# A hybrid encoder layer: order of the recurrence's drains, banks by result in its chunk step, and the key norm's root and reciprocal on tokens by heads

## The reference

```python
h = rms_norm(x, pre_mix_g);  z = h @ w_in          # 2048 -> 7296 columns
ya = neighbourhood_attention(...)                  # 8 heads of 64
yb = rwkv7_mixer(...)                              # 12 heads of 64, both directions
yc = retention_mixer(...)                          # 6 heads of 128
x = x + rms_norm(concat(ya, yb, yc) @ w_out, post_mix_g)
x = x + rms_norm(square(relu(rms_norm(x, pre_mlp_g) @ w_up)) @ w_down, post_mlp_g)
```

```python
kk = k * k_k;  kk = kk / max(sqrt(sum(kk * kk over 64 channels)), 1e-12)
# per token, state 64 x 64 per head and direction
sa = state @ (-kk)
state = state * w + outer(sa, kk * a) + outer(v, kd);   y = state @ r
```

## Time and profile before

| | us |
|---|---|
| median of 3 runs | 1355.91 |
| the runs | 1347.48, 1356.33, 1355.91 |
| profiled execution, its own time | 1349.03 |
| its span, first to last instruction | 1347.2 |
| PE busy / DVE / ACT / POOL | 1293.1 / 837.8 / 650.2 / 308.1 |

### The profile page before, as it was taken

One profiled execution on the slowest core, in us unless ns is written; L12 is line 12 of the kernel. 1 busy time (PEld: TensorE's weight loads), 2 busy tenths in 40 slices (PEclk: granted clock), 3 DMA queues, 4 the chain that ended last, 5 costly groups with the idle time before them and its releaser, 6 DMA issues.

```text
span 1347.2 us, 25329 instructions
## 1 busy us (share of the span) xinstructions
PE 1293.1 (96%) x10465; PEld 1132.2 (84%) x10465; DVE 837.8 (62%) x1179; ACT 650.2 (48%) x992; POOL 308.1 (23%) x255
## 2 busy tenths in 40 slices
PE   6999999999999899998999999999999999999996
PEld 5999888888899888877888888888888888888885
DVE  5566788888885976547555555555555545555455
ACT  5465654566434446447444444444444444444443
POOL 0011333243305121000455544444430000000000
PEclk9999999999999999998999999999999999999999
DMA  8666433233349334764766666666666666666663
GB/s 258 182 171 176 121 97 97 80 82 94 108 109 214 103 110 126 261 223 125 225 192 191 189 189 189 191 192 191 190 189 195 194 191 196 191 191 198 190 195 116
DMA packets 285751, 226.44 MB, mean 168 GB/s; under 512 B 15236, under 2 KB 263300, under 8 KB 284740
## 3 DMA queue, kind: packets, MB, share of 16 engines
q1 hardware_dynamic: 285168, 223.57, 56.8%
q0 software_dynamic: 240, 1.18, 0.3%
q10 hardware_dynamic: 228, 0.07, 0.0%
HBM read 222.69 MB, written 2.10 MB: 167 GB/s over the span
## 4 chain that ended last, share of the span: by engine, by line
PE 83%; DVE 8%; ACT 5%; issue 3%; DMA 1%; ACTq 0%; DVEq 0%
PE psum L2086 31%; PE psum L1733 18%; PE psum L1734 9%; PE psum L1722 7%; PE psum L1723 6%; PE psum L1724 6%; DVE w_lo L777 2%; ACT w_hi L1327 1%; PE psum L1865 1%; DMA raw<-in_w_out 1%; PE psum L1850 1%; PE psum L1789 1%; PE psum L1928 0%; PE psum L2141 0%; DVE arena L851 0%
## 5 line engine op out<-in xcount | busy, mean ns | idle before, releaser
L777 DVE TENSOR_TENSOR w_lo<-raw,w_hi 128x1024 fp32r<-128x1024 f32 x394 | 495.0, 1259 | 402.2 <-ACT w_hi L1327 401.3
L1327 ACT ACTIVATE w_hi<-raw 128x1024 fp32r<-128x1024 f32 x394 | 418.8, 1066 | 457.6 <-PE psum L2086 213.3
L1733 PE MATMUL psum<-act_both,w_hi 128*128 128x512 f32 x1024 | 355.4, 394 | 0.0
L2086 PE MATMUL psum<-w_hi,act_both 128*128 128x512 f32 x1216 | 327.4, 390 | 4.5 <-DVE act_both L1280 2.7
L1734 PE MATMUL psum<-act_both,w_lo 128*128 128x256 f32 x1024 | 283.8, 277 | 0.0
L1722 PE MATMUL psum<-act_both,w_hi 128*128 128x256 f32 x912 | 271.6, 298 | 7.5 <-DVE w_lo L777 6.1
L2086 PEld LDWEIGHTS psum<-w_hi,act_both 128*128 128x128 f32 x1216 | 227.7, 188 | 53.3 <-DVE act_both L1280 3.1
L1723 PE MATMUL psum<-act_both,w_hi 128*128 128x256 f32 x912 | 258.1, 283 | 0.0
L1724 PE MATMUL psum<-act_both,w_lo 128*128 128x256 f32 x912 | 257.8, 283 | 0.0
L1733 PEld LDWEIGHTS psum<-act_both,w_hi 128*128 128x128 f32 x1024 | 192.0, 187 | 44.6 <-DVE w_lo L777 0.2
L1734 PEld LDWEIGHTS psum<-act_both,w_lo 128*128 128x128 f32 x1024 | 192.3, 188 | 0.0
(11 more groups left out here) (235 smaller groups left out, 1076.0 us busy)
## 6 DMA issues: line engine op xcount, KB each, us to landing
raw<-in_w_up SPq DMA_DIRECT2D x128, 512.0 KB, 4.1
raw<-in_w_down SPq DMA_DIRECT2D x128, 512.0 KB, 4.2
raw<-in_w_in SPq DMA_DIRECT2D x114, 512.0 KB, 4.3
raw<-in_w_out SPq DMA_DIRECT2D x32, 512.0 KB, 4.5
arena<-in_x SPq DMA_DIRECT2D x2, 1024.0 KB, 6.1
arena<-in_na_rpb SPq DMA_DIRECT2D x16, 128.0 KB, 4.7
arena<-in_x SPq DMA_DIRECT2D x1, 2048.0 KB, 10.8
out_x<-arena SPq DMA_DIRECT2D x4, 512.0 KB, 2.7
```

The lines of the kernel that those rows point to most:

```text
L777: dve.tensor_tensor(by_half(h, low(h)), by_pair(h, raw[:, h % RAW]), by_half(h, high(h)).bitcast(F32), ALU.subtract).then_inc(s["lo_half"], 1)
L1327: act.activation(by_half(h, high(h)), by_pair(h, raw[:, h % RAW]), ACT.Copy).then_inc(s["hi_half"], 1)
L1733: pe.matmul(bank[b].rearrange("p (a t) -> p a t", a=2), wh, act_both[:, :, kt], start=kt == 0, stop=False)
L2086: last = pe.matmul(bank[4 * t + 2 * j + b], lhs[:, tokens], w[:, b * 512:(b + 1) * 512], start=start, stop=stop)
```

## The change

- **Key norm.** The squares become the stationary operand and two columns of ones (one for each head) the moving one, so that the sums come out as 128 tokens by 2 heads, twice (256 tokens): four columns in place of 256. ACT's root, DVE's maximum and reciprocal (`kk_factor`, a step of its own) work on 128x4. Four matmuls with the factor column, broadcast to 64, as stationary operand and the identity as moving one spread the factors over each head's channels into unused columns of bank 5 (`kk_wide`); DVE's norm multiplies by that. `make_p` of level 0 waits for the norm, since both touch bank 5.
- **Chunk step.** Bank 0 holds g of both heads and bank 1 y of both. One ACT copy takes g, one ACT copy or one DVE addition takes y.
- **Levels.** DVE adds both directions, does its chunk step, and then transposes both (`turn_q`). On ACT the last level's inverse is drained ahead of `between` (the exponentials of direction 1).
- **Order and place.** The copy of the chunks' end decays goes from DVE to ACT (`again`), and ACT's `decays` waits for `again_ready`. On DVE the chunk's fourth step comes ahead of the norm; it is now empty there.

Cut out of the diff are the semaphores' names, `feed`'s list lengths, and repeated renamings of `gy[e]` to `g_ps` and `y_ps`.

```diff
@@ -206,6 +206,7 @@
         LORA_BANK = [2, 4]
+        kk_wide = bank[5].rearrange("p (a t) -> p a t", a=2)[:, :, P:T]
         scores = psum[:, 2:4].rearrange("p e (t k) -> p e t k", t=TT)
...
@@ -256,7 +257,7 @@
         bn = cut(X2 + 1792, T)
-        kk_ss = bn
+        kk_f = small[:, 244:244 + 2 * TT]
         tmp = cut(16640, T)
...
@@ -398,9 +399,9 @@
                 if t < RW_CT - 1:
-                    square, root, lora, norm = feed(t + 1)
+                    square, root, factor, lora, norm = feed(t + 1)
                     tl = tilde(t + 1, 1 - p)
-                    early = [(root,), (), (norm, lora), (tl[0],)]
+                    early = [(root,), (factor,), (lora, norm), (tl[0],)]
                     between = [(tl[1],), (), (), (), (tl[4],)]
...
@@ -435,7 +436,7 @@
         PE_STARTS = {15: "root", 19: "lora"}
-        STARTS = {12: "square", 18: "root", 20: "norm", 21: "lora", 26: "sums_0", 29: "keys_0",
+        STARTS = {12: "square", 17: "root", 18: "factor", 20: "norm", 21: "lora", 26: "sums_0", 29: "keys_0",
                   31: "sums_1", 33: "keys_1"}
...
@@ -826,16 +827,20 @@
             def feed(t):
+                def kk_factor():
+                    dve.wait_ge(s["kk_root"], t + 1)
+                    nxt(dve.tensor_scalar(kk_f, kk_f, 1e-12, None, ALU.max))
+                    dve.reciprocal(kk_f, kk_f).then_inc(s["kk_factor"], 1)
+
                 def kk_norm():
-                    dve.wait_ge(s["kk_root"], t + 1)
+                    dve.wait_ge(s["kk_spread"], t + 1)
                     dve.wait_ge(s["kb_ready"], 2 * t)
                     dve.wait_ge(s["query_ready"], 2 * t)
-                    nxt(dve.tensor_scalar(kk_ss, kk_ss, 1e-12, None, ALU.max))
-                    nxt(dve.reciprocal(kk_ss, kk_ss))
-                    dve.scalar_tensor_tensor(kkn, zk[:, t], small[:, 48 + t:49 + t], kk_ss, ALU.mult,
-                                             ALU.mult).then_inc(s["kk_ready"], 1)
-
-                return [nothing] * 3 + [kk_norm]
+                    dve.scalar_tensor_tensor(kkn.rearrange("p (a t) -> p a t", a=TT),
+                                             zk[:, t].rearrange("p (a t) -> p a t", a=TT), small[:, 48 + t:49 + t],
+                                             kk_wide, ALU.mult, ALU.mult).then_inc(s["kk_ready"], 1)
+
+                return [nothing, nothing, kk_factor, nothing, kk_norm]

...
@@ -860,8 +865,6 @@
                     dve.wait_ge(s["exp_ready"], 6 * t + (3 * d + 3))
-                    last_t = C - 1 if d == 0 else 0
-                    dve.tensor_copy(ec[p][:, d], chunks(e_inc)[:, :, last_t])
                     dve.wait_ge(s["kd_ready"], 2 * t + (d + 1))
...
@@ -924,8 +927,8 @@
                 gap()
+                steps[3]()
                 run(early[2])
-                steps[3]()
                 gap()
...
@@ -953,6 +956,10 @@
                     z_new = new_columns(zd[:, half], d, n)
                     dve.tensor_tensor(z_new, packed(q_ps, n), z_new, ALU.add).then_inc(s["zd_ready"], 1)
+
+                def turn_q(d):
+                    if n == len(LEVELS) - 1:
+                        return
                     dve.wait_ge(s["zd_ready"], 10 * t + (2 * (n + 1) + d + 1))
                     if d:
...
@@ -967,17 +974,15 @@
                 run(steps[1:])
+                turn_q(0)
+                turn_q(1)
                 gap()
...

-                gy = [bank[e][:, 0:2 * C].rearrange("p (d v) -> p d v", d=2) for e in range(2)]
+                g_ps, y_ps = (bank[e][:, 0:2 * C].rearrange("p (d v) -> p d v", d=2) for e in range(2))
                 both = slice(n, 2 * NC - n, 2 * NC - 1 - 2 * n)
-
-                def g():
-                    dve.wait_ge(s["gy_done"], 4 * b + (n + 1))
-                    dve.tensor_copy(gs[C:P], gy[1][C:P]).then_inc(s["g_high"], 1)

...
@@ -1007,14 +1012,13 @@
                     order = slice(NC - 1 - n, n + 1, 2 * n - NC + 1)
-                    dve.tensor_tensor(y_i[0:C, order], gy[1][0:C], y_i[0:C, order], ALU.add)
-                    dve.tensor_tensor(y_i[C:P, order], gy[0][C:P], y_i[C:P, order], ALU.add).then_inc(s["y_added"], 1)
+                    dve.tensor_tensor(y_i[:, order], y_ps, y_i[:, order], ALU.add).then_inc(s["y_added"], 1)

...

-                return g, u, state_and_y
+                return nothing, u, state_and_y

...
@@ -1390,8 +1394,8 @@
                     act.wait_ge(s["kk_summed"], t + 1)
-                    act.wait_ge(s["tilde_ready"], 2 * t)
-                    act.activation(kk_ss, bank[2][:, 0:T], ACT.Sqrt).then_inc(s["kk_root"], 1)
+                    act.wait_ge(s["kk_spread"], t)
+                    act.activation(kk_f, bank[2][:, 0:2 * TT], ACT.Sqrt).then_inc(s["kk_root"], 1)
                     if t == 0:
...
@@ -1423,6 +1427,7 @@
                     act.wait_ge(s["query_ready"], 2 * t + d)
+                    act.wait_ge(s["again_ready"], 2 * t + d)
                     if d == 1:
...
@@ -1433,6 +1438,11 @@
                     act.wait_ge(s["query_ready"], 2 * t + (d + 1))
+                    if t >= 2:
+                        act.wait_ge(s["dec_ready"], 2 * (t - 1))
+                        act.wait_ge(s["s_ready"], 3 * (t - 1))
+                    last_t = C - 1 if d == 0 else 0
+                    act.activation(ec[p][:, d], chunks(e_inc)[:, :, last_t], ACT.Copy)
                     for v in (ar[p][:, d], bk[:, d]):
...
@@ -1475,21 +1485,24 @@
                 gap()
-                run(between)
                 if n == len(LEVELS) - 1:
...
                     take_inverse(1)
-                run(steps[1:])
+                    run(steps[1:])
+                    run(between)
+                else:
+                    run(between)
+                    run(steps[1:])
                 gap()
...
             def chunk(b, q, n):
-                gy = [bank[e][:, 0:2 * C].rearrange("p (d v) -> p d v", d=2) for e in range(2)]
+                g_ps, y_ps = (bank[e][:, 0:2 * C].rearrange("p (d v) -> p d v", d=2) for e in range(2))
                 both = slice(n, 2 * NC - n, 2 * NC - 1 - 2 * n)
...
                     act.wait_ge(s["gy_done"], 4 * b + (n + 1))
-                    act.activation(gs[0:C], gy[0][0:C], ACT.Copy).then_inc(s["g_low"], 1)
+                    act.activation(gs, g_ps, ACT.Copy).then_inc(s["g_ready"], 1)

...
@@ -1502,8 +1515,7 @@
                     order = slice(n, NC - n, NC - 1 - 2 * n)
-                    act.activation(y_i[0:C, order], gy[1][0:C], ACT.Copy)
-                    act.activation(y_i[C:P, order], gy[0][C:P], ACT.Copy).then_inc(s["y_copied"], 1)
+                    act.activation(y_i[:, order], y_ps, ACT.Copy).then_inc(s["y_copied"], 1)

...
@@ -1757,7 +1769,19 @@
                     pe.wait_ge(s["lora_free"], 4 * t)
-                    pe.matmul(bank[2][:, 0:T], ones, kk_sq, start=True, stop=True).then_inc(s["kk_summed"], 1)
+                    for a in range(TT):
+                        last = pe.matmul(bank[2][:, 2 * a:2 * a + 2], kk_sq[:, a * P:(a + 1) * P], ones[:, 0::C],
+                                         start=True, stop=True)
+                    last.then_inc(s["kk_summed"], 1)
+
+                def spread():
+                    pe.wait_ge(s["kk_factor"], t + 1)
+                    for a in range(TT):
+                        for e in range(2):
+                            last = pe.matmul(kk_wide[e * C:e * C + C, a],
+                                             kk_f[:, 2 * a + e:2 * a + e + 1].broadcast_to([P, C]), ident, start=True,
+                                             stop=True)
+                    last.then_inc(s["kk_spread"], 1)

...
@@ -1772,8 +1796,9 @@
                     last.then_inc(s["lora_done"], 1)
-
-                return [nothing, kk_sum, lora, nothing]
+                    spread()
+
+                return [nothing, kk_sum, nothing, lora, nothing]

...
@@ -1844,6 +1869,8 @@
                     pe.wait_ge(s["zd_ready"], 10 * t + (2 * n + 2))
+                    if n == 0 and t < RW_CT - 1:
+                        pe.wait_ge(s["kk_ready"], t + 2)
                     for m, d, e, h, to in tiles():
...
@@ -1915,13 +1942,12 @@
                                 h = slice(e * C, e * C + C)
-                                last = pe.matmul(gy[e][h, at[d]], ar[q][h, d, cd[d], 2 * e * C:2 * e * C + C], state[h, d],
+                                last = pe.matmul(g_ps[h, at[d]], ar[q][h, d, cd[d], 2 * e * C:2 * e * C + C], state[h, d],
                                                  start=False, stop=True, skip_group_check=True)
...
                 def u():
-                    pe.wait_ge(s["g_low"], 4 * b + (n + 1))
-                    pe.wait_ge(s["g_high"], 4 * b + (n + 1))
+                    pe.wait_ge(s["g_ready"], 4 * b + (n + 1))
                     for d in range(2):
...
@@ -1933,7 +1959,7 @@
                                 h, o = slice(e * C, e * C + C), slice((1 - e) * C, (2 - e) * C)
```

(18 more changed lines are left out.)

## The result

| | us |
|---|---|
| before, median of 10 runs | 1350.78 (1347.48 to 1357.13) |
| after, median of 10 runs | 1344.69 (1338.38 to 1346.22) |
| ratio | 0.9929, 95% interval 0.9909 to 0.9949 |
| profiled execution after, its own time / span | 1340.59 / 1338.8 |

The direction doesn't hang on it: the slowest run of after, 1346.22, is faster than the fastest of before, 1347.48. The forecast was -8.2 us and 1343, the range 1334 to 1352.

The account below looks back on a forecast made before the run. TensorE, busy 281.96 of 300 us in the recurrence, was taken as the bound; -4.1 - 1.2 - 1.2 - 1.2 - 1.5 - 2.0 + 3.0 = -8.2 us, put at 1343 us, range 1334 to 1352.

Parts of the forecast that it names:

- the waits of `make_p` and of g: Sign for the next profile: TensorE's waits at the levels' `make_p` and the chunk's g fall under 1 us together.
- A: Last level, ScalarE: draining the inverse ahead of the exponentials wins 5.1 us, 1.0 given back; net -4.1 us.
- B: Chunk's g: one ScalarE copy over 128 partitions in place of one each on ScalarE and VectorE; -1.2 us.
- E: VectorE relief, mainly the short reciprocal: about 3.5 us less per turn, of which little reaches TensorE; -1.5 us.
- C: Levels: VectorE's both additions ahead of both transposes, so `make_p` waits less, transposes hidden; -1.2 us.
- D: VectorE's new state moves ahead of the transposes, so TensorE's g products wait less; -1.2 us.
- F: Key norm's new TensorE work: sums 0.5, spread 0.65 us a tile, +3.0 us; filling level-0 `make_p`'s wait, -2.0 us.
- G: Level-0 `make_p`: its new wait for the next tile's norm costs nothing; if late, 0.3 to 1 us in four turns.
- given back to VectorE: Rival: VectorE's weight split and mask drains come last instead; gain only 4 down to 1 us, 1348; chance 0.24.
- One bank, one after another: Rival: chunk matmuls of row halves writing one bank take turns; +19.5 us, net +11, 1363; chance 0.04.

Follow-up runs that it names:

- e7: Kernel after with VectorE's bonus product moved ahead of the first gap of the products; stretch 374.8 us, ratio to before 0.9892.
- e10: Kernel before with the last-level inverse drained ahead of the exponentials and the bonus product ahead of the first gap; stretch 382.1 us, ratio 0.9955.
- e9: e7 with VectorE's first u copy of a turn moved ahead of the second pair of masks; stretch 374.5 us, ratio to before 0.9923.
- e3: Kernel before with banks by result alone: g of both heads in one bank, y in the other; stretch 382.8 us, ratio 0.9983.
- e6: Kernel after with an extra, unused 128x256 reciprocal on VectorE ahead of each key norm; stretch 378.1 us, ratio to before 0.9919.
- e4: Kernel before with the key norm alone changed (short root and reciprocal, spread by four products); stretch 385.0 us, ratio 1.0008.
- e11: Kernel after, unchanged, run again; stretch 376.5 us, ratio to before 0.9900.
- e2: Kernel before with VectorE adding both directions, doing its chunk step, then transposing; stretch 383.5 us, ratio 0.9967.
- e5: Kernel after with the inverse drained behind the exponentials again on ScalarE; stretch 378.8 us, ratio to before 0.9913.

## Why the prediction was right, and where not

The direction, the size (-8.2; -9.6 with an interval of some 2.7 to either side) and the bound were right: TensorE's own idle time in the turns was the gain to be had (18.0 us, 6.8 left), and the other stages passed it on. Of the signs that it named, one was missed: the waits of `make_p` and of g are 0.5 + 0.7 us and not under 1. By its terms:

- **A, -4.1 net: mis-sized, -2.3.** The waits behind the drain went as forecast (5.6 to 0.4 with the whole change), but the give-back was put at 1.0 and is about 2.8 (5.1 less 2.3). I had named what is late next at the chunk's state alone; the masks and the bonus product, queued behind a weight split that waits for ScalarE, came too. Moving the bonus wins 1.7 back (e7, e10); for the rest, the masks' waits (1.3 us) and the u copy's are named by the lists and not tested apart, but for 0.3 by e9.
- **B with its share of E: mis-sized the other way.** 1.2 for the g copy, and VectorE's relief in all 1.5. The banks alone gave 3.3, of which the g copy's waits are 1.3 (2.3 to 1.0) and the last `make_q`'s 1.9 (3.1 to 1.2). I had allowed 1.0 for that wait with every part in place. In the turn of the earlier trace rows the chain there was VectorE's two additions of y (0.28 + 0.29), its weight split and its keys, ahead of L944, which ends at 223.12; in e3 one addition of 0.29 stands in that place, L944 ends at 222.07, and L1862 starts at 222.18 without a wait. ScalarE's copy of g over 128 partitions takes 0.28 us, over 64 it took 0.27, as assumed.
- **C and D, -2.4: -2.6.** Right, the hidden transposes included.
- **E, the reciprocal:** e6 prices it at 1.6 us in place, a fifth of its 8.8 us. Right in kind: VectorE is not last in most of a turn. The pieces put at 3.5 us per turn add up to about 4.1 (with 0.40 for each copy of the end decays); VectorE's busy time fell by 15.8 us in the five turns, within the 15 to 20 forecast.
- **F, +3.0 and -2.0: right**, 0.66 and 0.50 us per tile against 0.65 and 0.5, and 2.1 us of the wait filled (2.4 to 0.3, e4). The start of the stretch moved by 0.5 in e4, as the first tile's share has it.
- **G, nothing: right.** No wait on the norm in the kernel after; e6 shows the wait when the norm is 1.75 us later.

The rivals. That it would be given back to VectorE happened to A and, as far as the runs show, to nothing else. They speak for order in the queue rather than load: 8.8 us of VectorE's work added at the norm cost 1.6 (e6), and e7 got 1.7 by moving one instruction of 0.47 us. One bank, one after another: not so, by L1912 and L1929 of e3. The forecast counted all of y among the products of row halves; its rest, 16 of the 28 matmuls, uses column halves, so of the rival's price of 19.5 us 5.6 had no ground. The rule of the Trainium skill's "TensorEngine Tiling (Array Packing)", section "Gotcha 1: PSUM Pressure", that different row tiles cannot access one PSUM bank simultaneously, is contradicted by these two rows as it was by L1850's, as long as the two row halves write different partitions; no run here has them write the same ones.

Taken by single runs, A came out 1.8 us below its term, and B, E and F together, forecast at -1.2 - 1.5 + 1.0 = -1.7, gave -4.4 and 0.5 back at the start, -3.9 (e3 and e4). The two errors went opposite ways: that the sum came out near the measured change is in part luck.

The version that beats both is e7: stretch 374.8 against 376.5 and 386.1, time 0.9892 of before. Against the kernel after its gain, 0.1%, rests on the stretch alone, since the times don't separate them; e9's 0.3 more likewise.

## What to carry to other kernels

Where one engine is at 94% of a stage, list its idle time by what ends it: that list bounds the gain and names the edits. When a wait is removed, look at every instruction that stands on the next engine's queue between there and the following hand-over, and above all for one that waits for a third engine: work that doesn't need that wait goes ahead of it. A change of a few us is measured on a stretch between two marks of the trace, not on the whole time.

## What the runs showed of the hardware

**Two speeds of one stage at the full clock.** The times of before gather around 1349.5 and around 1355.8, and those of after from 1338 to 1341 and from 1343 to 1346. Of the 51 executions of before that were taken beside the experiments 22 lie in the lower group and 29 in the upper, and the mean granted clock is 0.9943 in both. From its first matmul to its last, the w_up stage, whose instructions are the same in all these kernels, took 355.3 to 356.3 us in seven of the profiles and 361.9 to 362.8 in the other six. In 300 us of it, before and e7:

```profile
650.00:950.00 300.00, 300.00 (x1733) 262.35 (x1732) 156.95 (x136) 128.10 (x136) 151.38 (x84) 1.00 0.68 194
```

```profile
650.00:950.00 300.00, 300.00 (x1700) 260.30 (x1700) 152.59 (x133) 125.50 (x133) 148.88 (x79) 1.00 0.66 190
```

TensorE is busy throughout at a granted clock of 1.00 in both, yet gets through 1.9% fewer matmuls in e7. Nothing waits, and it is no stall at one place: in windows of 50 us e11 gets through 290 or 291 matmuls each time and e7 through 285. The cause stays open; it is worth 6.6 us, two thirds of what the change saves.

**Dips of the clock.** The 0.96 of the turn before was this, at 273 us:

```profile
273.06:276.47 3.41, 3.41 (x21) 3.29 (x21) 3.35 (x5) 2.26 (x4) 2.00 (x2) 0.50 0.03 5
277.00:280.00 3.00, 3.00 (x45) 2.81 (x46) 1.97 (x5) 1.77 (x3) 0.68 (x1) 1.00 0.61 175
```

0.50 is 1.2 GHz in place of 2.4, with 21 matmuls in 3.4 us against 45 in 3.0. In before and e4 it follows TensorE's longest idle time in the turns, 1.7 us; e2, with 1.6 us at the same seam, has none. In e5 and e6 it lies at 445 us, behind a wait of 1.7 us for a weight split, and every other kernel here has that wait without a dip behind it. So the idle time before it does not settle it.

Over whole executions the mean granted clock is 0.9943 in 51 of before and 0.9956 in 14 of after: 0.0013 of 1345 us, about one dip of 1.7 us less. With it the account closes, as an estimate: -9.6 in the stretch, +0.9 ahead of it and -1.7 are -10.4 us, inside the 6.9 to 12.3 of the ratio. That the change as such makes dips rarer is not shown: e5 and e6, which hold most of it, are at 0.9942 (6 and 4 executions).

**Reciprocal.** 1753 ns for 256 columns, 278 for 20 and 178 for 4 (L833 after): 6.2 ns per column, where the product L839 of 256 columns takes 478 in all.
